# RWKV block: v projected inside the scan core as fp32 products, one unit per tile

## What is computed

```python
xx = x_prev - x                                   # token shift
xs = x[None] + xx[None] * mu[:, None, None, :]    # six mixes: r, k, v, w, a, g
rkv = jnp.einsum('nbtd,nde->nbte', xs[:3], w_rkv) # 1024 x 1024 each
r, k, v = rkv[0], rkv[1], rkv[2]
# decay from xs[3], rate a from xs[4], gate g from xs[5], by low-rank products
kk = normalised(k * k_k);  k = k * (1 + (a - 1) * k_a)
# per head of 64: S = S * w + (S a) b^T + v k^T ;  y = S r     (scan over tokens)
yn = groupnorm(y) * lnx_w + lnx_b
bonus = sum(r * k * r_k) * v
out = ((yn + bonus) * g) @ w_o
```

## Time and profile before

| | us |
|---|---|
| median of 3 runs (2660.79 to 2660.97) | 2660.92 |
| the profiled execution's own time | 2665.29 |
| its span in the trace | 2663.5 |
| PE busy | 2415.7 (91%) |
| DVE busy | 1367.5 (51%) |
| ACT busy | 989.0 (37%) |
| mean granted TensorE clock | 0.89 |

### The profile page before, as it was taken

How to read it: one execution, slowest core, us unless ns; L and a number is a source line. 1 busy time by engine, 2 the same in 40 slices (tenths; PEclk the granted TensorE clock), 3 DMA queues, 4 the chain that set the end, 5 groups by cost and what they waited for, 6 DMA issues and landing times.

```text
span 2663.5 us, 38389 instructions
## 1 busy us (share of the span) xinstructions
PE 2415.7 (91%) x14870; PEld 1819.4 (68%) x14870; DVE 1367.5 (51%) x2204; ACT 989.0 (37%) x1568; POOL 55.5 (2%) x84
## 2 busy tenths in 40 slices
PE   5988888887899999689999899999777899999998
PEld 3865666665688887454555688888454688788886
DVE  4465677663564644744443464545535443544444
ACT  4564333332442323344443452323334443432222
POOL 0001111110000000000000000000000000000000
PEclk8996887877999999876777999999886899999999
DMA  3210000003132322000001133232110133232321
GB/s 122 98 51 7 5 5 8 5 2 122 60 104 95 96 94 80 28 20 20 20 31 47 48 110 95 95 98 86 57 55 0 32 94 110 87 99 92 102 89 61
DMA packets 53830, 168.74 MB, mean 63 GB/s; under 512 B 6992, under 2 KB 12240, under 8 KB 53584
## 3 DMA queue, kind: packets, MB, share of 16 engines
q1 hardware_dynamic: 53712, 167.08, 19.5%
HBM read 164.96 MB, written 2.10 MB: 63 GB/s over the span
## 4 chain that ended last, share of the span: by engine, by line
PE 81%; DVE 12%; ACT 4%; issue 3%; DMA 0%; SPq 0%; DVEq 0%; ACTq 0%
PE bank L1452 59%; PE bank L1727 2%; PE bank L1471 2%; PE bank L1750 2%; PE bank L1569 2%; PE bank L1744 2%; PE bank L1730 1%; PE bank L1792 1%; PE bank L1588 1%; DVE rstd L832 1%; PE bank L1784 1%; PE bank L1609 1%; PE bank L1521 1%; PE bank L1806 1%; DVE tmp L861 1%
## 5 line engine op out<-in xcount | busy, mean ns | idle before, releaser
L1452 PE MATMUL bank<-a_hi,w_hi 128*128 128x512 f32 x1504 | 605.4, 403 | 42.9 <-DVE w_lo L826 20.6
L1452 PE MATMUL bank<-a_hi,w_lo 128*128 128x512 f32 x1504 | 590.7, 393 | 0.0
L1452 PE MATMUL bank<-a_lo,w_hi 128*128 128x512 f32 x1504 | 590.0, 392 | 0.0
L826 DVE TENSOR_TENSOR w_lo<-w_raw,w_hi 128x1024 fp32r<-128x1024 f32 (+3 forms) x336 | 371.7, 1109 | 318.9 <-ACT w_hi L458 313.2
L458 ACT ACTIVATE w_hi<-w_raw 128x1024 fp32r<-128x1024 f32 (+3 forms) x336 | 320.3, 958 | 181.2 <-PE bank L1452 179.5
L1452 PEld LDWEIGHTS bank<-a_hi,w_hi 128*128 128x128 f32 x1504 | 285.2, 190 | 123.8 <-issue 41.9
L1452 PEld LDWEIGHTS bank<-a_hi,w_lo 128*128 128x128 f32 x1504 | 285.7, 190 | 63.7 <-issue 6.8
L1452 PEld LDWEIGHTS bank<-a_lo,w_hi 128*128 128x128 f32 x1504 | 285.4, 190 | 60.3
L1452 PE MATMUL bank<-b_hi,w_hi 128*128 128x512 f32 x688 | 277.8, 404 | 18.2 <-DVE b_lo L884 18.1
L1452 PE MATMUL bank<-b_hi,w_lo 128*128 128x512 f32 x688 | 268.7, 391 | 0.0
L1452 PE MATMUL bank<-b_lo,w_hi 128*128 128x512 f32 x688 | 268.6, 390 | 0.0
(11 more groups left out here) (283 smaller groups left out, 3075.1 us busy)
## 6 DMA issues: line engine op xcount, KB each, us to landing
w_raw<-in_f0gu SPq DMA_DIRECT2D x44, 512.0 KB, 3.4
w_raw<-in_f1gu SPq DMA_DIRECT2D x44, 512.0 KB, 3.4
w_raw<-in_f2gu SPq DMA_DIRECT2D x44, 512.0 KB, 3.5
w_raw<-in_f0dn SPq DMA_DIRECT2D x16, 512.0 KB, 3.4
w_raw<-in_f1dn SPq DMA_DIRECT2D x16, 512.0 KB, 3.5
w_raw<-in_mix SPq DMA_DIRECT2D x16, 512.0 KB, 3.6
w_raw<-in_f2dn SPq DMA_DIRECT2D x16, 512.0 KB, 3.4
w_raw<-in_in SPq DMA_DIRECT2D x10, 512.0 KB, 3.4
```

The lines of the kernel that those rows point to most:

```text
L826: dve.tensor_tensor(w_lo[r][:, 0:n, :], raw[r][:, 0:n, :], w_hi[r][:, 0:n, :].bitcast(F32), ALU.subtract).then_inc(w_split[r], 1)
L1452: mm = pe.matmul(bank[r][:, :], w[r][:, k, :], a[:, k, :], start=(k == 0 and n == 0), stop=(k == kt - 1 and n == 2))
```

## The change

- The dense phase v is gone, and with it its weight splits and its mix as a pair of high and low parts. The operands of the later mixes swap buffers.
- During phase r, ACT and DVE also mix v's input, into `v_mix`, one fp32 buffer for all eight tiles where `v_t` lay.
- SP loads v's raw weight units in turn into two buffers `v_raw` while the core runs.
- `v_steps` makes v for a tile as eight fp32 products of 128x512 into bank 5, spread out: blocks 0 to 2 of tile j + 2 as half products of 256 tokens in the six scan steps of core(j); blocks 3 and 4 of tile j + 1 after level 1, block 5 after level 2, block 6 after level 3 ahead of the gate product, block 7 after level 4. Tile 0's and the first three of tile 1's run before the first front. The last core has none, the one before it none in its scan.
- ACT copies bank 5 to `v_s` after level 5 (`v_copy`). The gate goes straight to `z_t`.
- Bank 5 being taken, outputs go to banks 3 and 2, u to bank 6, scores (0, 1) and (0, 2) both to bank 6 with (0, 2) last and waiting for the mask of (0, 1). PE waits for the output's copy before `turn` into bank 2, and for `r_hat`'s first half before the inner output products.

```diff
-Y_BANKS = (3, 5)
-SCORES = ((0, 0), (0, 1), (0, 2), (1, 0), (1, 1), (1, 2), (1, 3), (0, 3))
+Y_BANKS = (3, 2)
+V_BANK = 5
+V_EARLY = 3
+SCORES = ((0, 0), (0, 1), (1, 0), (1, 1), (1, 2), (1, 3), (0, 3), (0, 2))
-    out = [("r", 8, (8,) * 4), ("k", 8, (8,) * 4), ("v", 8, (8,) * 4), ("lora", 4, (8,) * 4), ("w_o", 8, (8,) * 4)]
+    out = [("r", 8, (8,) * 4), ("k", 8, (8,) * 4), ("lora", 4, (8,) * 4), ("w_o", 8, (8,) * 4)]
-MIXES = {"r": (0, 0, "b"), "k": (1, 1, "a"), "v": (2, 2, "b"), "w1": (3, 3, "a"), "a1": (4, 4, "b"), "g1": (5, 5, "a")}
+MIXES = {"r": (0, 0, "b"), "k": (1, 1, "a"), "w1": (2, 3, "b"), "a1": (3, 4, "a"), "g1": (4, 5, "b")}
+V_MIX = 2
...
+            wait_evacuated(sp, "lora")
+            load_v(0)
+            load_v(1)
+            for j in range(1, DT):
                 sp.wait_ge(lora_done, j * 3)
                 load_tile(j)
+                if j + 1 < DT:
+                    sp.wait_ge(v_done, j)
+                    load_v(j + 1)
...
+            def v_base_of(j):
+                act.activation(tile(v_mix, j), tile(hp, j, 1, T + 1), ACT.Copy, scale=column(omu, V_MIX * DT, j))\
+                    .then_inc(v_based, 1)
...
+            def v_copy(q):
+                act.wait_ge(v_done, q + 1)
+                act.activation(v_s[:, :], bank[V_BANK][:, :], ACT.Copy).then_inc(vs_ready, 1)
...
+            def v_mix_of(j):
+                dve.wait_ge(v_based, j + 1)
+                dve.scalar_tensor_tensor(tile(v_mix, j), tile(hp, j, 0, T), column(vecs, VEC["mu"][0] + V_MIX * DT, j),
+                                         tile(v_mix, j), ALU.mult, ALU.add).then_inc(v_mixed, 1)
...
+            def v_steps(q, steps, lo=0, hi=T):
+
+                pe.wait_ge(v_loaded[q % 2], 16 * (q // 2 + 1))
+                pe.wait_ge(v_mixed, DT)
+                if q:
+                    pe.wait_ge(vs_ready, q)
+                for k in steps:
+                    mm = pe.matmul(bank[V_BANK][:, lo:hi], v_raw[q % 2][:, k, :], v_mix[:, k, lo:hi], start=(k == 0 and lo == 0),
+                                   stop=(k == DT - 1), skip_group_check=True)
+                if k == DT - 1:
+                    mm.then_inc(v_done, 1)
...
+                    if last is not None and b in Y_BANKS:
+                        pe.wait_ge(y_ready, last * 2 + 2)
                     turn(b, src)
...
                     if ahead and lv == 1:
+                        v_steps(q, range(V_EARLY, 5))
                         pe.wait_ge(x_ready2, j + 1)
                         key_norms(q)
                         decay_product(q)
                     elif ahead and lv == 2:
+                        v_steps(q, (5,))
                         rate_product(q)
                     elif ahead and lv == 3:
+                        v_steps(q, (6,))
                         gate_product(q)
+                    elif ahead and lv == 4:
+                        v_steps(q, (7,))
...
+                pe.wait_ge(rhat_ready, j * 2 + 1)
...
                         mm.then_inc(carried, 1)
+                        if j + 2 < DT:
+                            half = (ch - 1) % 2 * (T // 2)
+                            v_steps(j + 2, ((ch - 1) // 2,), half, half + T // 2)
...
             rate_product(0)
+            v_steps(0, range(4))
             gate_product(0)
+            v_steps(0, range(4, DT))
             bonus_sums(0)
+            v_steps(1, range(V_EARLY))
             front(0)
```

More of the change, by code:

```diff
@@ L249, in build @@
         hp = at("hp", [P, DT, T + 1], M0)
[L250 removed]
+        r_t, k_t, v_mix = at("r_t", [P, DT, T], R0), at("k_t", [P, DT, T], R0 + 8 * ROW), at("v_mix", [P, DT, T], X0)
         z_t = at("z_t", [P, DT, T], B0)
+        v_raw = [at(f"v_raw{i}", [P, DT, P], W0 + (20 + 2 * i) * ROW) for i in range(2)]
         lora_wa, lora_g0 = at("lora_wa", [P, T], L0), at("lora_g0", [P, T], L0 + ROW)
@@ L256, in build @@
         rows_free = iter([M0 + ROW * i for i in range(8)] + [A0 + ROW * i for i in range(16)]
-                         + [B0 + ROW * i for i in range(8, 16)] + [W0 + ROW * i for i in range(24)])
+                         + [B0 + ROW * i for i in range(8, 16)] + [W0 + ROW * i for i in range(20)])
+        half_rows = []
         def scratch(name, shape=(P, T)):
-            return at("rw_" + name, shape, next(rows_free))
+            if int(np.prod(shape[1:])) * 4 > ROW // 2:
+                return at("rw_" + name, shape, next(rows_free))
+            if not half_rows:
+                row = next(rows_free)
+                half_rows.extend((row + ROW // 2, row))
+            return at("rw_" + name, shape, half_rows.pop())
         (sig_w, cum, inv_decay, a_gate, k_sq, k_norm, k_clamp, k_inv, kk, a_dec, b_tok, b_dec, k_fac, k_new,
@@ L324, in build @@
             "gate_padded conv0 conv_done gate_act act_scaled hid_tmp hid_high")
+        v_loaded = [ctx.enter_context(nc.semaphore(f"v_loaded{i}")) for i in range(2)]
         (lora_loaded, lora_done, prep_step, near_ready, norm_step, ends_copied, sigw_ready, agate_ready, ggate_ready, ksq_ready, vs_ready,
@@ L404, in load_ffn @@
                     load(f"{tag}dn{p}")
-            for name in ("r", "k", "v", "lora"):
+            for name in ("r", "k", "lora"):
                 load(name)
@@ L410, in load_tile @@
                     .then_inc(lora_loaded, 16)
-                if not isinstance(j, int):
+                if j:
                     sp.wait_ge(bonus_ready, j)
@@ L553, in _ @@
             read_out("r", lambda i, r: act.activation(tile(r_t, SLOTS * i + r), bank[r][:, :], ACT.Copy), "k")
-            read_out("k", lambda i, r: act.activation(tile(k_t, SLOTS * i + r), bank[r][:, :], ACT.Copy), "v")
-            read_out("v", lambda i, r: act.activation(tile(v_t, SLOTS * i + r), bank[r][:, :], ACT.Copy), "w1")
+            read_out("k", lambda i, r: act.activation(tile(k_t, SLOTS * i + r), bank[r][:, :], ACT.Copy), "w1")
             mix_tiles("a1")
@@ L595, in prep_decay @@
                 act.wait_ge(lora_done, q * 3 + 3)
-                act.wait_ge(vs_ready, q + 1)
-                act.activation(tile(v_t, q), bank[3][:, :], ACT.Copy).then_inc(ggate_ready, 1)
+                act.activation(tile(z_t, q), bank[3][:, :], ACT.Copy).then_inc(ggate_ready, 1)
             def natural_copy(q, n):
@@ L640, in core @@
                             prep_decay(j + 1)
+                        else:
+                            v_copy(j + 1)
                 act.wait_ge(wu_done, j * 2 + 1)
@@ L649, in _ @@
             prep_decay(0, True)
+            v_copy(0)
             for n in range(4):
@@ L1483, in _ @@
             norm("n_mix")
-            for phase in ("r", "k", "v"):
+            for phase in ("r", "k"):
                 q, _, src = MIXES[phase]
                 dense(phase, lambda r: opnd[src], lambda r, k: pe.wait_ge(mix_low, q * DT + k + 1))
-            dense("lora", lambda r: opnd["aba"[min(r, 2)]],
+            dense("lora", lambda r: opnd["bab"[min(r, 2)]],
                   lambda r, k: pe.wait_ge(mix_low, (MIXES["w1"][0] + min(r, 2)) * DT + k + 1))
@@ L1604, in core @@
                 pe.wait_ge(x_ready2, j + 1)
-                for b, src in ((4, a_nat), (5, x_nat)):
+                for b, src in ((4, a_nat), (6, x_nat)):
                     for c in range(TT):
```

32 lines of the change are left out of this document (21 added, 11 removed).

## The result

The changed kernel takes **2600.87 us** (median of 4 runs, 2599.49 to 2601.35) against 2660.94 before: ratio 0.9769, 95% interval 0.9752 to 0.9786. The forecast was 2603. The sum came out near; its terms did not all, and the clock did more than I gave it. The runs of the kernel before lie near 2661 and near 2665.5, and the profiled execution is one of the latter (2665.29), so the traces differ by 64.5 us where the medians differ by 60.1.

What follows compares the result with a forecast made beforehand. PE bounds the kernel (busy 2415.7 of 2663.5 us), its core stretched by a mean clock of 0.77. Terms -43.4 + 4.5 + 18.1 + 3 - 40.5 = -58 us give 2607 by profile, 2603 by median; range 2580 to 2648 us.

Steps and rivals of the forecast that it cites:

- last step: End of the sum: runs' median lies 4.4 us below the profiled execution, so 2607 by the profile becomes 2603 us.
- the 4 us given back in the first core: First core, levels 1 to 3: low clock costs 5.5 us more there, of which 4 come back.
- Dense phase: Phase v removed: eight units of 5.43 us, -43.4 us; the extra mix in phase r costs 0.
- Price of a product: Each added 128x512 fp32 product: 1.03 us at full clock, about 2.0 at 1.2 GHz; prologue's eleven products +4.5 us.
- Levels 1 and 2: Core, two products after level 1 (+1.55) and one after level 2 (+1.03): 2.6 x 7 tiles, +18.1 us.
- Scan: Six half products per scan, tiles 0 to 5: at most +0.12 a step, 0.08 taken, +3 us in all.
- scan steps over 1 us: Core's scan: a named sign of being wrong; steps of 0.75 to 0.85 us were expected.
- Levels 3 and 4, banks and waits: Core: one product each after levels 3 and 4 hides, cost 0; banks and waits 0 to +0.5 us a tile.
- Clock: Core: 128-row products raise the clock in levels 4 and 5, behind scans and in the first core: -40.5 us.
- rival A: Full clock throughout the core but for the last tile: clock terms 58 us, total -76, 2585 us; chance 0.25.
- Rival B: The core's clock keeps its pattern, no clock terms: -10 to -1 us, 2651 to 2660 us; chance 0.18.
- Rival C: Slower, 2678 us: scan, levels 1 and 2 at 1.2 GHz; turns once half products exceed PE's free 0.4 us; chance 0.04.

Runs made afterwards that it cites:

- the banks alone: Kernel before with only the changed kernel's banks and waits (outputs, u, scores moved), v still a dense phase: 2661.21 us, ratio 1.0003.
- the quarter products: Changed kernel with the scan's half products cut from 256 to 128 columns, leaving out part of v: 2592.76 us, ratio 0.9735.

## Why the prediction was right

The mechanism was right; four terms were mis-sized, and the time came out as near as it did in part by luck. By the traces the change is -64.5 us against the sum's -58, so the forecast by the profile, 2607, missed by 6 us. Its last step takes off 4.4 us, by which the median before lay below the profiled execution, and so comes to 2603; but the changed kernel's profiled execution (2600.76) lies at its median. The 4.4 us seem to be a matter of the first core: with the banks alone, where the profiled execution took 2660.32, that core takes 47.4 us from its first scores to its output copy, and in the profiled kernel before 51.8. If so, the forecast counted them twice, once among the 4 us given back in the first core and once in the last step.

- *Dense phase*: -43.4 forecast, -43.2 measured. The extra mix in phase r cost nothing that shows: by the landmarks the stretch before the core lost just the phase, within the 1 to 2 us by which that landmark moves.
- *Price of a product*: 1.03 us forecast. It holds for one that stands between 64-row products (1.06), not for a row of them (0.885). The 1.03 of the earlier trace rows was read from such a place. In the prologue that makes +2.3 us instead of +4.5. The four passes that the Trainium skill gives (FP8 and Floating Point Precision, TensorE Precision Notes), 0.90 by my estimate from a dense product's pace, were the better guide for the rows of products; the trace agrees with 0.885.
- *Levels 1 and 2*: +18.1 forecast. In the third core level 1 grew by 1.2 us and level 2 by 1.05, 2.25 a tile, +16 for seven.
- *Scan*: +3 forecast, 36 x 0.29 = +10.4 measured. The step that failed is "It is 0.52 if cost goes by columns", with the 0.12 a step that bounded it: the half product takes 0.63, of which 0.21 does not go by columns (the quarter products), and the small groups are 0.38 and not 0.32. The bound from above was too low. A step of 1.01 us also meets one of the signs of being wrong that the prediction named, "scan steps over 1 us"; it told of this term, and the clock stayed high in the scans. (Of the others, a wait for v's weights came too, of 0.15 us; the tile period is 45.4 us, where 45 or less was forecast.)
- *Levels 3 and 4, banks and waits*: 0 forecast. The gate product still waits 0.29 us, level 5 still 0.81, and the banks alone measured 2661.21 us against 2661.31.
- *Clock*: -40.5 forecast. The core lost 23.2 us; with +16 and +10.4 put back, the clock gave 23.2 + 16 + 10.4 = 49.6 by difference, between the forecast and rival A's 58 (about 45 if the 4.4 us above are left out). I had left a low piece in levels 4 and 5 of many tiles; one piece of 7 us in the first core (192.5 to 199.5) and one of 3.5 behind the seventh scan are all that is left ahead of the last core. From the gate product to the scan the third core lost 5.7 us, near the bound of 6.3.

Rival A was thus nearly right on the clock's pattern, and missed the time by 16 us: 8.4 us are clock that it counted and the kernel did not get back, 7.4 the scan and 4.4 the last step, both of which it shared with me; the prologue and levels 1 and 2 came out 4.3 us cheaper. Rival B is about what happens when the same products stand elsewhere: 2649.23 us. Rival C did not come up; the scans ran at full clock, yet its turning point was met in another way: the half product did cost more than PE had free in a step, at 2.4 GHz.

That the clock answers to the 128-row products put in, and to their places, is shown by three runs in which they are added (core clock 0.79 to 0.87, 0.80 to 0.96, and 0.50 to 1.00 in the last core), one in which they are left out (0.83), and two in which they are moved (0.93, 0.83). PE busy for 95% with 64-row products stayed at 0.50 for 17 us in the last core, so a high busy share did not raise the clock there. The rule of the Trainium skill (TensorE: Matmul & The Clock Gate, Part 1), that activity releases the throttle, agrees as far as the added products go, and does not tell of such a stretch. What about a 128-row product counts, its rows, its columns or its length, was not separated. One rival stays open: each product also fills a wait of PE, so that small products in the same waits might have kept the clock up too. No run puts 64-row work there.

## What to carry to other kernels

Look at the granted clock beside PE's busy share before you judge added PE work. In this kernel, where many small products with short waits ran at 1.2 GHz, a large product put into the wait paid for itself, and the place mattered more than the amount (same products, 48 us apart). Put such work where the timeline shows PE waiting for another engine, one piece per wait, and not in a row behind one of them. In a chain of short steps, price the insert from a row with the same neighbours, and expect a fixed part (0.21 us here). Before you add a profile's offset to the runs' median to a forecast, ask where in the profile it lies; a term may hold it already.

## What the hardware showed that I had not expected

- Seven useless fp32 products of 128x512 made the kernel 16 us faster, the work of 53 of them some 21 us.
- A 128-row fp32 product between 64-row ones holds PE for 0.42, 0.63 and 1.06 us at 128, 256 and 512 columns; the same in a row of its like takes 0.885 at 512.
- In the last core five useless 128x512 products kept 17 us at full clock that otherwise ran at half; in the traces that core got 2.3 us shorter.
